# Attention line of a streaming encoder step: probabilities turned three units behind the scores instead of two

## What is computed

```python
# A: latent attention (8 heads), B: forgetting attention (8 heads), C: attention into 256 memory tokens (4 heads)
s = (einsum('bqhd,bkhd->bhqk', q_nope, k_nope) + einsum('bqhr,bkr->bhqk', q_rope, k_rope)) * MLA_SCALE
p = masked_softmax(s, chunk_mask);            o_mla = einsum('bhqk,bkhd->bqhd', p, v_mla)
s = einsum('bqhd,bkhd->bhqk', f_q, f_k) * FOX_SCALE + (c_q - c_k)     # c: running sums of log forget values
p = masked_softmax(s, causal);                o_fox = einsum('bhqk,bkhd->bqhd', p, f_v)
s = einsum('bqhd,bmhd->bhqm', m_q, m_k) * MEM_SCALE
p = softmax(s);                               o_mem = einsum('bhqm,bmhd->bqhd', p, m_v)
y = sum_i gates[i] * (o_i @ w_br[i]);         mix = y @ w_out
gates = sigmoid(h @ w_in[:, gate columns])    # 3072 columns, computed beside the attention
# ... residual, layer norm, router, 64 experts (top 8) and a shared expert, residual, layer norm
```

## Time and profile before

| | us |
|---|---|
| median of 3 runs | 1324.92 (1320.33 to 1329.11) |
| the profiled execution's own time | 1329.72 |
| its span, first to last instruction | 1327.9 |
| attention, first exponential to first branch projection | 197.6 to 538.7 |
| prompt part, up to the first scores of the sample | up to 365.9 |
| sample part | 365.9 to 538.7 |

### The profile page before, as it was taken

One profiled execution on the slowest core, in us unless ns is written; L12 is line 12 of the kernel. 1 busy time (PEld: TensorE's weight loads), 2 busy tenths in 40 slices (PEclk: granted clock), 3 DMA queues, 4 the chain that ended last, 5 costly groups with the idle time before them and its releaser, 6 DMA issues.

```text
span 1327.9 us, 17493 instructions
## 1 busy us (share of the span) xinstructions
PE 1236.7 (93%) x6418; PEld 679.5 (51%) x6418; DVE 597.8 (45%) x1511; ACT 155.4 (12%) x333; POOL 44.1 (3%) x53
## 2 busy tenths in 40 slices
PE   6889999999899998999896999999999999999994
PEld 4445545554455555434473555555555555555541
DVE  2230014665676755333544444444444444444436
ACT  1101211111211111001110100111110100111113
POOL 0100000000000000000000000000000000000000
PEclk9899999999999988999887999999999999999997
DMA  8141052220243424686410899999999999999991
GB/s 296 55 162 63 15 203 87 80 88 16 80 164 124 150 87 154 207 337 251 140 50 24 341 393 382 379 381 371 375 386 378 379 395 388 381 380 380 371 364 50
DMA packets 82291, 308.98 MB, mean 233 GB/s; under 512 B 13920, under 2 KB 19456, under 8 KB 56128
## 3 DMA queue, kind: packets, MB, share of 16 engines
q1 hardware_dynamic: 67136, 275.01, 52.8%
q0 software_dynamic: 5696, 15.47, 4.0%
q10 hardware_dynamic: 9408, 17.83, 3.8%
HBM read 302.25 MB, written 10.74 MB: 236 GB/s over the span
## 4 chain that ended last, share of the span: by engine, by line
PE 87%; DVE 6%; issue 4%; DMA 2%; ACT 1%; DVEq 0%; ACTq 0%; SPq 0%
PE ps_P L1174 17%; PE ps_V L1199 9%; PE ps_V L1188 9%; PE ps_P L910 8%; PE ps_P L816 7%; PE ps_S L1188 4%; PE ps_T L809 4%; PE ps_P L824 3%; PE ps_V L1127 3%; PE ps_V L1118 3%; PE ps_T L1163 3%; PE ps_P L1068 2%; DMA small<-gates 2%; PE ps_S L919 1%; PE ps_V L1151 1%
## 5 line engine op out<-in xcount | busy, mean ns | idle before, releaser
L1174 PE MATMUL ps_P<-arena,branch_out 128*64 128x256 f32 (+1 forms) x2176 | 233.6, 379 | 0.5 <-DVE branch_out L1790 0.5
L1174 PEld LDWEIGHTS ps_P<-arena,branch_out 128*64 128x64 f32 (+1 forms) x2176 | 151.3, 136 | 90.7 <-issue 19.1
L910 PE MATMUL ps_P<-weight_ring,xT 128*128 128x512 f32 x288 | 137.5, 605 | 0.0
L1796 DVE TENSOR_TENSOR branch_out<-branch_out,ps_P 128x256 f32<-128x256 f32 x33 | 13.9, 421 | 266.2 <-PE ps_P L1174 266.2
L1188 PE MATMUL ps_V<-weight_ring,branch_out 128*128 128x512 f32 x264 | 124.2, 593 | 0.0
L1199 PE MATMUL ps_V<-arena,branch_out 128*64 128x512 f32 (+1 forms) x544 | 120.6, 599 | 0.0
L1817 DVE TENSOR_TENSOR x_sb<-x_sb,ps_V 128x512 f32<-128x512 f32 x136 | 93.6, 688 | 23.9 <-PE ps_V L1188 17.3
L1351 ACT ACTIVATE weight_ring<-ps_V,merge 128x512 f32<-128x512 f32 x66 | 45.3, 687 | 427.5 <-PE ps_V L1199 427.5
L910 PEld LDWEIGHTS ps_P<-weight_ring,xT 128*128 128x128 f32 x288 | 51.2, 194 | 41.6 <-issue 41.2
L1188 PEld LDWEIGHTS ps_V<-weight_ring,branch_out 128*128 128x128 f32 x264 | 48.1, 192 | 47.3 <-issue 47.3
L1188 PE MATMUL ps_S<-weight_ring,branch_out 128*128 128x512 f32 x132 | 67.4, 592 | 0.0
(11 more groups left out here) (307 smaller groups left out, 1326.4 us busy)
## 6 DMA issues: line engine op xcount, KB each, us to landing
arena<-w_e_gate SPq DMA_DIRECT2D x68, 1024.0 KB, 8.4
arena<-w_e_up SPq DMA_DIRECT2D x68, 1024.0 KB, 10.5
arena<-w_e_down SPq DMA_DIRECT2D x68, 1024.0 KB, 7.3
weight_ring<-w_in SPq DMA_DIRECT2D x12, 1024.0 KB, 8.3
weight_ring<-w_in ACTq DMA_DIRECT2D x8, 1024.0 KB, 6.2
gates<-arena ACTq DMA_DIRECT2D x18, 256.0 KB, 2.1
small<-gates ACTq DMA_DIRECT2D x18, 256.0 KB, 3.2
arena<-cache_fox_k SPq DMA_DIRECT2D x8, 512.0 KB, 3.9
```

Source lines behind the costliest of these rows:

```text
L910: last = mm(out[:, :], xT[:, k, j * P:(j + 1) * P], slot[:, k % 4, :], start=(k == 0), stop=(k == KD - 1))
L1174: last = mm(bank[r:r + wide, 0:256], xgT[q][:, k, r:r + wide], w[h][:, k, :], start=(k == 0), stop=(k == KD - 1))
```

## The change

Turning the probabilities (`T p`) moves from two steps behind the scores to three, the value product from three to four, and the last product of a unit from four to five. The loop of `plan()` gets one step more. `prob` gets a fourth buffer, and the exponential waits for the turn of unit n - 4 instead of n - 3. Nothing else in the list moves: `S`, `load_keys`, `prep`, the gate pieces and `norm` stay in their steps. SP's list and its waits are not edited.

```diff
-    for n in range(n_u + 4):
+    for n in range(n_u + 5):
...
         if 1 <= n <= n_u:
             s.append(("norm", n - 1))
-        if 2 <= n <= n_u + 1:
-            s.append(("T", "p", n - 2))
         if 3 <= n <= n_u + 2:
-            s.append(("V", "o", n - 3))
-        if n >= 4 and U[n - 4][0] == "mla":
-            s.append(("V", "ov", n - 4))
-        elif n >= 4 and U[n - 4][1] == "s":
-            s.append(("T", "o", n - 4))
+            s.append(("T", "p", n - 3))
+        if 4 <= n <= n_u + 3:
+            s.append(("V", "o", n - 4))
+        if n >= 5 and U[n - 5][0] == "mla":
+            s.append(("V", "ov", n - 5))
+        elif n >= 5 and U[n - 5][1] == "s":
+            s.append(("T", "o", n - 5))
...
-        prob = [Y.take(T) for _ in range(3)]
+        prob = [Y.take(T) for _ in range(4)]
...
-                    if n >= 3:
+                    if n >= 4:
 
-                        act.wait_ge(done["T"], done_at("T", "p", n - 3))
-                    fn(prob[n % 3][0:rows, 0:nk * P], ps["S"][n % 2][0:rows, 0:nk * P], ACT.Exp, bias=mx[0:rows, n:n + 1],
+                        act.wait_ge(done["T"], done_at("T", "p", n - 4))
+                    fn(prob[n % 4][0:rows, 0:nk * P], ps["S"][n % 2][0:rows, 0:nk * P], ACT.Exp, bias=mx[0:rows, n:n + 1],
```

More of the change, by code:

```diff
@@ L1006, in _ @@
                         for t in range(nk):
-                            last = tr(out[:, t * P:t * P + rows], prob[n % 3][0:rows, t * P:(t + 1) * P], rows)
+                            last = tr(out[:, t * P:t * P + rows], prob[n % 4][0:rows, t * P:(t + 1) * P], rows)
                     elif key[0] == "o":
@@ L1687, in _ @@
                     link(V.reciprocal(rs[0:rows, n:n + 1], sm[0:rows, n:n + 1]))
-                    pv = prob[n % 3][0:rows, 0:nk * P]
+                    pv = prob[n % 4][0:rows, 0:nk * P]
                     V.tensor_scalar(pv, pv, rs[0:rows, n:n + 1], None, ALU.mult).then_inc(norm_ready, 1)
```

## The result

The longer line is slower: 1342.3 us in the median (1339.9 to 1343.3, 4 runs) against 1325.1 us (1320.3 to 1329.1), a ratio of 1.0129 with a 95% interval of 1.0092 to 1.0165. That is +17.2 us, between 12 and 22. Forecast were +14.3 us, 1339 us, in a range of 1330 to 1349.

A forecast was written before the change was run, and what follows sets the result against it. It took PE, busy 93% of the span, as the bound, counting DVE only where PE waits. Terms -0.2 - 0.2 + 9.7 + 5.0 = +14.3 us on the 1324.9 us median gave 1339.2 us, range 1330 to 1349 (8 in 10).

The forecast's parts named there:

- its largest term: New PE waits at T clat for the late latent load in streams 2 to 7: +9.7 us, bounds 5 and 15.
- Part 1: PE's eight waits for normalised probabilities (L1689, 5.5 us) pass to value products; gain 0.2 us, bounds 5.5 and 0.
- Part 2: Fourth prob buffer: the exponential waits for the turn of unit n - 4; cost 0, gain 0.
- Part 3: Line starts a step later and ends a step later; -0.2 us, bounds -1.7 and +1.7.
- From there on all is shifted and unchanged: Sign to look for in the profile: from the first branch projection on, everything is only shifted.
- Part 4: Latent load issued a step later, T clat stays: 4 x 2.1 + 2 x 0.67 = 9.7 us of waits.
- which leaves 2.1 - 1.43 = 0.67 us each: Streams 5 and 6: the new T clat wait absorbs 1.43 us of PE's waits just behind it.
- The wait of 1.25 us at 509.23: PE wait in the sample part, taken as unchanged because it hangs on a gate product that moves along.
- The other loads: L675, L678, L681 and the first branch weights move with their readers and all stay covered.
- Part 5: Sample part: new waits bring 1.6 more falls of the granted clock at 3.1 us, 5.0 us; bounds 0 and 18.6.

The follow-up runs named there:

- the run with the prompt alone: Kernel before with the longer line and fourth buffer for units 0 to 35 only: 1327.0 us, ratio 1.0017.
- both cures: Changed kernel with a third latent buffer and the small turn T o ahead of the gate piece: 1325.4 us, ratio 0.9989.
- with the reciprocal last: DVE's gate part (L1628, L1629) moved last in its step: changed kernel with third latent buffer 1303.1 us, kernel before 1303.5 us.
- the late load alone: Kernel before, only the latent load of stream b waits one step longer, for the fox unit's value product: 1331.3 us, ratio 1.0038.
- changed, third buffer: Changed kernel with a third latent and rotary key buffer, so stream b waits for stream b - 3: 1332.4 us, ratio 1.0052.
- changed, small turn early: Changed kernel with a sample unit's small turn T o ahead of its step's gate piece, latent load left late: 1334.0 us, ratio 1.0060.

## Why the prediction came out as it did

The sum was near, +14.3 against +17.2, and its largest term was the right one. Two of its terms were near partly by luck, as parts 4 and 5 say. Step by step:

**Part 1, the waits for L1689: right.** They passed to the value products. These waits are longer than the old ones (6.9 us against 5.5, where I had written about 4), because PE is done with the turn before it waits; the value product starts no earlier. The gain of 0.2 us can't be seen: up to the sample part PE stood still for 1.3 us more in all. The fourth buffer and the prompt's longer line win nothing (the run with the prompt alone), and neither does the whole longer line (both cures: 1325.4; with the reciprocal last: 1303.1 against 1303.5).

**Part 2: nothing speaks against it.** No run tests the fourth buffer by itself; PE's instruction count is the same, and the runs with the longer line and without its side effects take the time of the short line.

**Part 3, the ends: right within its bounds.** The prompt part ended 1.5 us earlier where I had said within 1, the drain's wait is 3.1 us instead of 3.9, and the runs with both causes removed leave nothing of the sum. "From there on all is shifted and unchanged" did not hold in this pair of executions, which differ by 2.6 us behind the attention.

**Part 4, the latent load: right in mechanism, wrong for streams 5 and 6.** For streams 2, 3, 4 and 7 I had 4 x 2.1 = 8.4 us; measured were 8.3. That the sum is so close is luck: three waits were 0.3 us shorter than 2.1 and the one of stream 2 was 0.8 us longer. The step that failed is "which leaves 2.1 - 1.43 = 0.67 us each". The 1.43 us did vanish, but the wait was 3.63 us and not 2.1, so 2.2 us each, 3.1 us more for both. I had followed the operands of `T clat` and its load, and had not written out the T ring of step 53 anew, where a `T o` had come in and a turn behind the reciprocal had got the bank. The wait of 1.25 us at 509.23, which I had left as it is, shrank to 0.44 us (at 527.07). The other loads stayed covered, as forecast: no other DMA is named among PE's waits.

**Part 5, the clock: right in sign, and near in size partly by luck.** I had forecast 1.6 falls more, at 3.1 us each, 5.0 us. There were three more, six instead of three (I had counted only the two ahead of the drain), but four of the six last 3.4 us and not 6.8. The time at the lower level rose from 17 to 27 us. At 3.1 us for 6.8 such us the 10 us more are an estimated 4.6 us; PE's busy time over the whole attention, which leaves out the work that moved from one part to the other, rose by 3.7 us.

Both waits of 3.63 us had a fall behind them in this execution (470.7 and 494.6), and so had two waits for the load, of 1.77 and 1.85 us (446.8 and 518.4); those of 2.89 and 1.81 us had none. I had priced falls by the number of waits; the runs say that the number is a poor guide: the late load alone brought six more waits and no time beyond them. Counted in the same way, one execution of each, the sample part spent about this long at the lower level:

| kernel | us at the lower level |
|---|---|
| before | 17 |
| late load alone (six waits for the load) | 17 |
| changed (four waits for the load, two for the bank) | 27 |
| changed, third buffer (the two bank waits are left) | 17 |
| changed, small turn early (six waits for the load) | 10 |
| changed, both | 7 |

In both pairs that differ by the small turn's place, 17 or 10 us at the lower level go with the two bank waits. The medians over all runs point the same way: the mean clock over the span was 0.969 before, 0.969 with the late load alone and with both cures and 0.970 with the small turn early, and 0.963 and 0.964 in the two kernels with the bank waits. But the longer line for the prompt alone had 0.965 without any of them, and lost 1 us, so the bank waits are not the only thing that moves the clock.

In all, in the profiled execution, the sample part grew by 17.7 us. PE stood still for 11.2 us more: 8.3 for the four load waits and 4.4 for the two bank waits less what vanished, less 0.8 at 509.23 and 0.8 at the drain. It was busy for 6.5 us more, of which 2.8 us had left the part ahead of it and 3.7 us go with the clock.

## What to carry to other kernels

When a step of a software pipeline is moved later, everything that is released by it moves too: find every buffer that another queue refills behind it, and count the work between the new release and the next use, here 0.6 us against 2.7 us of issue and landing. Write out the ring of banks anew for each kind of step, since a shifted entry changes who holds the bank two places earlier. And where a wait names the last instruction of a queue, look at what is at the head of that queue: moving the 3.35 us reciprocal behind the short copies won 22 us in a kernel where a longer line won none. A cure can bring waits of its own: list the waits again after each edit.

## What was not expected of the hardware

The falls of the clock are not proportional to waiting: in the sample part the granted clock was 0.95 with six more waits of 1.2 to 2.4 us (the late load alone), as without them, and 0.93 with two waits of 3.6 us among the six. It was 0.95 again with those two alone (the third buffer), in the fastest execution of that kernel. What makes one wait of 1.8 us end in a fall and another not stays open. The latent load's wait for the same 160 KB differed from place to place, 1.77 to 2.89 us in one execution and up to 3.1 us in another. Stream 2 has no small turn between the product and the scores, which is part of why its wait was the longest; the rest stays open.
